# Sparse attention: the value products of four heads in one matmul, and one copy out for four results

## What is computed

```python
logits = jnp.einsum('bthc,btjc->bthj', qb, kv_sel) * (KV_LATENT ** -0.5)
logits = logits + bias            # by distance and head
logits = jnp.where(valid[:, :, None, :], logits, -jnp.inf)
p = jax.nn.softmax(logits, axis=-1)
o = jnp.einsum('bthj,btjc->bthc', p, kv_sel)
return o.reshape(Bsz, Q_BLOCK, hq) @ w_out
```

## Time and profile before

| | us |
|---|---|
| median of three runs | 3058.54 (3057.65 to 3058.82) |
| the profiled execution | 3051.9 |
| its span | 3050.1 |
| the stage in it, first logits to last result copied | 2216.4 to 2334.5 |
| TensorE busy over the span | 2700.7 (89%) |
| VectorE busy | 1088.2 (36%) |
| ScalarE busy | 700.3 (23%) |

### The profile page before, as it was taken

How to read it: one execution, slowest core, us unless ns; L and a number is a source line. 1 busy time by engine, 2 the same in 40 slices (tenths; PEclk the granted TensorE clock), 3 DMA queues, 4 the chain that set the end, 5 groups by cost and what they waited for, 6 DMA issues and landing times.

```text
span 3050.1 us, 51036 instructions
## 1 busy us (share of the span) xinstructions
PE 2700.7 (89%) x20889; PEld 2064.3 (68%) x20889; DVE 1088.2 (36%) x2208; ACT 700.3 (23%) x1213; POOL 170.5 (6%) x209
## 2 busy tenths in 40 slices
PE   6999999999899999997778887898988967877887
PEld 6888884755578888776566666664466745666666
DVE  4555542222442234446311111146355552111114
ACT  3121331044232234222200000022065330000001
POOL 0100001000000000000000000302000001000002
PEclk8999999999999999998899999998999979999999
DMA  7655432311223223231199999942200018999993
GB/s 236 191 173 179 151 117 93 97 56 56 70 83 97 96 90 104 79 101 56 72 422 422 422 422 422 416 149 103 81 15 15 17 80 360 422 422 422 422 422 144
DMA packets 206765, 594.29 MB, mean 195 GB/s; under 512 B 9472, under 2 KB 133584, under 8 KB 157264
## 3 DMA queue, kind: packets, MB, share of 16 engines
q1 hardware_dynamic: 202880, 575.47, 49.2%
q0 software_dynamic: 3504, 16.63, 1.7%
q10 hardware_dynamic: 288, 0.89, 0.1%
HBM read 590.79 MB, written 7.41 MB: 196 GB/s over the span
## 4 chain that ended last, share of the span: by engine, by line
PE 68%; DMA 21%; DVE 6%; issue 2%; ACT 1%; SPq 1%; DVEq 0%; ACTq 0%
PE bank L1743 29%; DMA ring<-in_exp_w 21%; PE bank L2103 8%; PE bank L2186 5%; PE bank L1833 4%; PE bank L1956 4%; PE bank L1925 3%; PE bank L2077 2%; PE bank L2155 2%; PE bank L1914 1%; PE bank L2275 1%; PE bank L2004 1%; PE bank L1687 1%; SPq L472 1%; DMA ring<-in_w_ada 1%
## 5 line engine op out<-in xcount | busy, mean ns | idle before, releaser
L1743 PE MATMUL bank<-parts 128*128 128x512 f32 x2624 | 816.9, 393 | 22.5 <-DVE parts L1067 10.3
L2103 PE MATMUL bank<-ring,arena 128*64 128x256 f32 x4096 | 495.8, 392 | 179.4 <-DMA ring<-in_exp_w 178.8
L1743 PEld LDWEIGHTS bank<-parts 128*128 128x128 f32 x2624 | 492.8, 189 | 125.0 <-issue 22.4
L2103 PEld LDWEIGHTS bank<-ring,arena 128*64 128x64 f32 x4096 | 329.2, 135 | 309.5 <-issue 202.8
L1743 PE MATMUL bank<-parts,ring_low 128*128 128x512 f32 x1312 | 512.9, 391 | 0.0
L1061 DVE TENSOR_TENSOR ring_low<-ring,parts 128x2048 fp32r<-128x2048 f32 x96 | 215.2, 2245 | 204.4 <-ACT parts L689 204.1
L1743 PEld LDWEIGHTS bank<-parts,ring_low 128*128 128x128 f32 x1312 | 247.9, 189 | 52.3
L1513 DVE SCALAR_TENSOR_TENSOR arena<-arena,bank 128x128 f32<-128x128 f32 x128 | 44.2, 345 | 656.3 <-ACT arena L826 656.3
L2121 PEld LDWEIGHTS bank<-arena,ring 128*64 128x64 f32 x8192 | 266.0, 138 | 16.5 <-ACT arena L667 1.1
L2121 PE MATMUL bank<-arena,ring 128*64 128x64 f32 x8192 | 263.3, 222 | 0.7 <-ACT arena L667 0.7
L689 ACT ACTIVATE parts<-ring 128x2048 fp32r<-128x2048 f32 x96 | 179.8, 1873 | 237.6 <-DMA ring<-in_w_ffn_in 110.9
(11 more groups left out here) (316 smaller groups left out, 2670.7 us busy)
## 6 DMA issues: line engine op xcount, KB each, us to landing
ring<-in_exp_w SPq DMA_DIRECT2D x384, 1024.0 KB, 10.3
ring<-in_w_ffn_in SPq DMA_DIRECT2D x44, 1024.0 KB, 5.5
ring<-in_w_ada SPq DMA_DIRECT2D x36, 1024.0 KB, 5.5
ring<-in_w_ffn_out SPq DMA_DIRECT2D x20, 1024.0 KB, 5.1
ring<-in_w_in SPq DMA_DIRECT2D x18, 1024.0 KB, 5.1
ring<-in_conv_w_in SPq DMA_DIRECT2D x12, 1024.0 KB, 5.2
ring<-in_attn_w_in SPq DMA_DIRECT2D x10, 1024.0 KB, 9.4
ring<-in_attn_w_out SPq DMA_DIRECT2D x8, 1024.0 KB, 5.1
```

The lines of the kernel that those rows point to most:

```text
L1743: i = mm(o, a[:, cols[0], cols[1]], b, start=first_ and n == 0, stop=last_ and n == 2)
L2103: x = mm(bank[s][64 * f:64 * f + 64, 0:2 * P].rearrange("p (w n) -> p w n", w=2), XW[:, s, k], ring[:, 3 * s:3 * s + 2, c0:c0 + 2 * P - 1: ...
```

## The change

The turned probabilities no longer go to `PT2` but to `PT4`, a view of `U` as two buffers of four key blocks with 512 columns each: in key block `j` the 128 queries of four heads lie side by side. `probs(u)` is a unit's part in it, `qb + 1` blocks of 128 columns, 512 apart. PE makes a value product once in four steps (`i % 4 == 2`), for the four heads together: `qb + 1` matmuls with the same stationary operands and 512 columns, into a whole bank 4 or 5. VectorE copies the four results out at once, in the step after. The arithmetic of each result is the same, in the same order of key blocks.

```diff
+        PT4 = U[:].rearrange("p k s -> p (k s)").rearrange("p (g j n) -> p g j n", g=2, j=TT)
...
-        PT2 = area(24576, 2, SEQ)
...
+        def probs(u):
+
+            qb, h = u // HEADS2, u % HEADS2
+            return PT4[:, u // 4 % 2, 0:qb + 1, P * (h % 4):P * (h % 4) + P]
...
                     if u % 2 == 0:
                         act.wait_ge(sem("att_tp"), ATT["tp"] + u + 1)
-                        if u:
-                            act.wait_ge(sem("att_pv"), ATT["pv"] + u - 1)
-                    if u % 2 == 0:
-                        A_(PT2[:, 0, 0:n], bank[2][:, 0:n], ACT.Copy).then_inc(sem("att_pt"), 1)
-
-            act.wait_ge(sem("att_y"), ATT["y"] + 64)
+                        if u >= 8:
+                            act.wait_ge(sem("att_pv"), ATT["pv"] + u // 4 - 1)
+                        A_(probs(u), bank[2][:, 0:n].rearrange("p (j q) -> p j q", q=P), ACT.Copy)\
+                            .then_inc(sem("att_pt"), 1)
+
+            act.wait_ge(sem("att_y"), ATT["y"] + 16)
...
-            for i in range(len(units) + 3):
+            for i in range(len(units) + 4):
...
-                if i >= 2 and i % 2:
+                if i >= 2 and i % 2 and i - 2 < len(units):
                     u = i - 2
                     n = (units[u][0] + 1) * P
                     dve.wait_ge(sem("att_tp"), ATT["tp"] + u + 1)
-                    if u >= 2:
-                        dve.wait_ge(sem("att_pv"), ATT["pv"] + u - 1)
-                    nc.vector.tensor_copy(PT2[:, 1, 0:n], bank[3][:, 0:n]).then_inc(sem("turned_odd"), 1)
-                if i >= 3:
-                    u = i - 3
-                    qb, h = units[u]
-                    dve.wait_ge(sem("att_pv"), ATT["pv"] + u + 1)
-                    nc.vector.tensor_copy(Q2[:, h, qb * P:qb * P + P], bank[4 + u % 2][:, 0:P])\
-                        .then_inc(sem("att_y"), 1)
+                    if u >= 8:
+                        dve.wait_ge(sem("att_pv"), ATT["pv"] + u // 4 - 1)
+                    nc.vector.tensor_copy(probs(u), bank[3][:, 0:n].rearrange("p (j q) -> p j q", q=P))\
+                        .then_inc(sem("turned_odd"), 1)
+                if i >= 4 and i % 4 == 3:
+                    g = i // 4 - 1
+                    qb, h = units[4 * g]
+                    dve.wait_ge(sem("att_pv"), ATT["pv"] + g + 1)
+                    nc.vector.tensor_copy(Q2[:, h:h + 4, qb * P:qb * P + P],
+                                          bank[4 + g % 2][:].rearrange("p (h q) -> p h q", h=4)).then_inc(sem("att_y"), 1)
...
-                if i >= 3:
+                if i >= 3 and i % 4 == 2:
                     u = i - 3
-                    qb = units[u][0]
+                    g, qb = u // 4, units[u][0]
+                    turned(u - 1)
                     turned(u)
-                    if u >= 2:
-                        pe.wait_ge(sem("att_y"), ATT["y"] + u - 1)
+                    if g >= 2:
+                        pe.wait_ge(sem("att_y"), ATT["y"] + g - 1)
                     for j in range(qb + 1):
-                        x = mm(bank[4 + u % 2][:, 0:P], CKV[:, j], PT2[:, u % 2, P * j:P * j + P],
-                               start=(j == 0), stop=(j == qb))
+                        x = mm(bank[4 + g % 2][:], CKV[:, j], PT4[:, g % 2, j], start=(j == 0), stop=(j == qb))
                     x.then_inc(sem("att_pv"), 1)
-            pe.wait_ge(sem("att_y"), ATT["y"] + 64)
+            pe.wait_ge(sem("att_y"), ATT["y"] + 16)
```

## The result

The changed kernel took 3066.3 us (median of 8 runs, 3064.0 to 3072.1), the kernel before in the same runs 3058.2 (3055.4 to 3059.1): 8.1 us more, ratio 1.0030 with a 95% interval of 1.0019 to 1.0041. Two later sets gave 1.0043 (1.0030 to 1.0056) and 1.0047 (1.0033 to 1.0061), 13 to 14 us. The profiled execution has a span of 3063.0 us against 3050.1. So it is slower, as forecast, but by 8 to 14 us and not by 18.5, and the first median lies just under the range of the forecast (3067 to 3085).

What follows compares the result with a forecast made beforehand. The prediction took the sparse attention stage as bound by a latency loop through PE, VectorE and ACT. Its terms, 13.8 + 2.2 + 2.5 = +18.5 us, put the median at 3077 us, range 3067 to 3085.

Steps and rivals of the forecast that it cites:

- What bounds the stage: Sparse attention stage: a latency loop through PE, VectorE and ACT sets the pace, one value product in each two-head pass.
- The 4.01 us of the pass without product: Last quarter: a two-head pass of 4.99 us with its one value product taken off.
- The gain set against it: PE busy time of the value products: 34.4 us instead of 49.7, a gain only if the stage waits for PE.
- the 34 named as a sign: Sign that the forecast is right: the value products' matmul records fall to some 34 us.
- The value products: Each burst is added whole to two passes without product, plus 0.11 us: +13.8 us over the stage's loop.
- The copy term: VectorE's 128x512 result copy behind each burst delays the next maximum: 0.17 us a group, +2.5 us; ends 0 and 10.4.
- The tail: End of the stage: last burst and larger result copy delay ACT's splitting of the output weights, +2.2 us.
- Its own range of 12 to 24: The loss's range by the ends, in us: latency on either side of the result copy's cost, slower probability copies 0 to +2.
- carrying the sum over to the median: The profiled execution lies 6.6 us below the timed median; this was taken to carry over, 3058.5 + 18.5 = 3077 us.
- 1 (bursts covered, faster): Stage keeps its pace during bursts and PE was the bound: -10 us, 3048.5 us; chance 5%.
- 2 (half covered): Work ahead hides bursts in the first three quarters; only three last-quarter groups lose, 4.8 us, 3063.3 us; chance 8%.
- 3 (clock): PE idles longer between short passes, so the first quarter runs at half clock: +8 us, 3085 us; chance 8%.

Runs made afterwards that it cites:

- copy_later: The changed kernel with the 128x512 result copy two steps later on VectorE; ratio to the kernel before 1.0043, stage 132.0 us.
- burst_small: The changed kernel with each 512-column matmul of a burst made as four of 128 columns, same place; ratio to the kernel before 1.0044, stage 134.2 us.
- product_mid: The kernel before with each head's 128-column value product and result copy one step later, the product between logits and transposes; 3042.6 us, ratio 0.9952.
- spread_mid: The changed kernel with its 512-column matmuls spread, at most one a step, between logits and transposes; 3047.9 us, ratio to the kernel before 0.9967.

## Why the prediction was right in kind and wrong in size

**What bounds the stage: right for three quarters of four.** It said that the passes through PE, VectorE and ACT set the pace and not PE's work. The burst in another place gave 12 us back with the same matmuls, and products off the passes made the stage 11 us shorter than before with no instruction less. For the quarter with 384 keys the busy share (31.29 of 32.40 us) was the wrong row to read, as the prediction had it: the chain there goes through VectorE and ACT. For the last quarter it was wrong: with 37.91 of 38.00 busy, PE was the bound before, and its chain holds both products of a pair of heads and not one. The 4.01 us of the pass without product came from taking one of them off. That this is also the length of the pass through ACT (4.00 in the chain of after) is luck: the two loops tie, 4.98 us of PE's work against 4.01 + 0.98. It was the burst that made the pass the bound there, as the prediction had it for all quarters. In the first three quarters the subtraction is sound.

**The gain set against it: misread.** "15 us less" compares the recorded busy time of the small products (49.7 us, each record with its modelled end) with the columns' time of the large ones (80 x 0.43). The columns' time before was 320 x 0.107 = 34.2 us, the same as after, and the records came to 39.6 us and not to the 34 named as a sign. So even where PE is the bound only the 0.11 us beside each small product was to be gained, and not 15 us.

**The value products: right, a little large.** Forecast groups of 4.61, 6.93, 9.23 and 11.57 us; measured 4.60, 6.81, 9.12 and 11.44. The excess from the second quarter on is the 0.11 us that each burst was given beyond 0.43 a record; the chain shows bursts of 1.72, 2.58 and 3.44 us, bare columns. Over 15 bursts the groups' excess is 1.4 of the 13.8 us.

**The copy term: wrong.** 2.5 us were taken for the maximum that starts late behind the 128x512 copy. The maximum does start late. But what stands behind it on ACT ends almost in time for the next pass: the chain runs for a stretch over the copy, the maximum and ACT's queue, and then comes out at the same group time as without it (copy_later: 6.82 against 6.81, 9.12 against 9.12). The durations had been added end to start; on VectorE the next instruction starts up to 0.1 us before the last one's end (copy 2288.46 for 0.68, maximum at 2289.05 in the trace of copy_later). The lower end, 0, was the right one. The loop from the first to the last maximum grew by 11.7 us (110.9 to 122.7), not by 13.8 + 2.5 = 16.3. The copy term is 2.5 of the difference, the bursts 1.4, and about 0.8 is that before had a longer group (6.45 for 6.17, 8.34 for 8.08) at three turns of a quarter, which after has not.

**The tail: mis-sized the other way.** Forecast +2.2; measured from the last maximum to the end of the stage 10.4 against 6.5, +3.9. 1.8 of it are the last burst at a lower clock, 5.36 for 3.60 us; at full clock burst_small had a tail of 8.9. The rest, 2.1, is what was forecast. The prediction had weighed a clock fall for the first quarter alone.

**The sum for the stage** was then 18.5 against 15.7, and 16.2 in the mean of three traces each. Its own range of 12 to 24 doesn't follow from the ends that it names: with the copy term at 0 the sum is 16.0, and with every upper end it is 31. Measured is the lower end, plus 1.8 for the clock fall and less the 1.4 of the bursts and the 0.8 at the turns.

**The steps that failed: the copy term, and carrying the sum over to the median.** The forecast was +18.5 and the medians gave +8.1. Of the 10.4 us between them 5.6 are missing in the profiled executions already (12.9 apart): 2.8 in the stage, by the terms above, 2.1 for its earlier start and 0.6 behind it. The other 4.8 are the step to the median. The prediction took the profiled execution of before to lie 6.6 us under the timed ones and let that difference carry over to the changed kernel. It doesn't: in the runs with the result before lay 6.3 us under its median and after 1.5 under its own. The profiled execution of before had the full clock for most of the 110 us behind the stage, and seven of the eight timed ones of before lay in the upper crowd near 3058; of the changed kernel's eight, six had a mean granted clock of 0.969 to 0.971 and took 3064 to 3067, two had 0.967 and took 3071 and 3072. So 8.1 us were measured for a stage that loses 16, by chance of which executions fell together. In the two later sets, with before spread over both crowds and after near 3069 to 3071, it was 13 to 14. Why an execution falls in one crowd or the other stays open; that the pause 75 us behind the stage is where they part is seen in the traces, not proved by an experiment that takes the pause away. Also not shown is why the ratios, 13 to 14 us, stay below the stage's 16.2. The start of the stage is no reason: it came 2.1 us earlier than before's in the first pair of traces and 2.3 and 2.5 later in the others. The intervals (9 to 19 us) do not exclude 16.

**The rivals.** 1 (bursts covered, faster): fell with the groups of after. But it was right that PE was the bound of the last quarter, and its groups (3.64, 5.10, 7.2, 9.44) are near those of product_mid (3.9, 5.1, 7.3, 9.7): what it needed were products in the covered place. Its own sum is -3.1 a group and not -3.0. 2 (half covered): fell as a mechanism, since the three shorter quarters lost 0.8, 1.7 and 3.3 us in the trace, although the first measured median, 3066.3, lay close to its 3063. 3 (clock): the second to fourth quarters had 1.00; only the start (0.91, 0.82 and 0.91 in the three traces) and the last burst did not.

## What to carry to other kernels

In a loop over several engines, write down the pass that returns to the same engine and count what stands on it. Merging matmuls, copies or anything else into one run helps only if the run lies in time in which the other engines have work in hand; at the head of a pass the whole run is added. Moving a step behind the instructions that feed the others can gain more than making it smaller: here the same products, moved one place, took 11 us off the stage (0.5% of the whole with what followed), while merging them into bursts cost 16. And a busy share doesn't name the bound: with PE busy 97% of the third quarter the chain went through VectorE and ACT, with 99.8% in the last it was PE alone. Read the chain in each stretch, and count which products are on it.

## What the runs showed of the hardware

- A float32 matmul of 512 columns takes two records of 0.43 us; sixteen records of 128 columns on the same engine take 1.79 us in place of 1.72. Width hardly matters when the stream is unbroken: 4% there, and 3.57 against 3.44 us for the bursts of the last quarter.
- The Trainium skill (Perfetto Trace Analysis, Matmuls) has it that larger matmuls are more efficient when possible. The traces agree by little: 3.44 against 3.57 us for the same burst, and, where PE was the bound, 9.54 (one group) against 9.68 us for four heads in the last quarter of spread_mid and product_mid, 1.4%. Put at the head of a pass, the same matmuls made the stage 14% longer (133.4 against 117.1 us), ten times as much.
- A PE pause of 3.34 us with the same work around it was followed by a granted clock of 0.57 in one execution and 1.00 in another, worth 2.8 us there; with a second such difference 30 us later and small ones beside them the two ended 7.3 us apart behind the stage. One profiled execution is therefore no base for a change of a few microseconds.
